# Pairing the 512-column and the 256-column products of the up projections

## What is computed

```python
def swiglu(u, w_in, w_out):
    a, b = jnp.split(u @ w_in, 2, axis=-1)          # 1024 -> 2 x 2816
    return (jax.nn.silu(a) * b) @ w_out
h = h + 0.5 * swiglu(rms_norm(h, ffn1_norm), ffn1_w_in, ffn1_w_out)   # ffn1, later ffn2
def squared_relu_mlp(h, w1, w2):
    return jnp.square(jax.nn.relu(h @ w1)) @ w2      # 1024 -> 4096, mlp0 and mlp1
```

## Time and profile before

| what | value |
|---|---|
| median of 3 runs | 1203.59 us |
| the profiled execution's own time | 1205.99 us |
| its span | 1204.2 us |
| TensorE busy | 1192.3 us (99%), 7787 matmuls |
| VectorE busy | 868.6 us (72%) |
| ScalarE busy | 646.5 us (54%) |
| GpSimd busy | 220.7 us (18%) |
| mean granted TensorE clock | 0.995 of full speed |

### The profile page before, as it was taken

One profiled execution on the slowest core, in us unless ns is written; L12 is line 12 of the kernel. 1 busy time (PEld: TensorE's weight loads), 2 busy tenths in 40 slices (PEclk: granted clock), 3 DMA queues, 4 the chain that ended last, 5 costly groups with the idle time before them and its releaser, 6 DMA issues.

```text
span 1204.2 us, 19499 instructions
## 1 busy us (share of the span) xinstructions
PE 1192.3 (99%) x7787; PEld 1063.5 (88%) x7787; DVE 868.6 (72%) x1199; ACT 646.5 (54%) x868; POOL 220.7 (18%) x110
## 2 busy tenths in 40 slices
PE   9999999999999999999999999999999999999997
PEld 6888888988899888888999988888899878888886
DVE  6877667788868877766788786665688777766553
ACT  6655544475655755545643554544446684555441
POOL 1443301000000234310000025410000240554000
PEclk9999999999999999999999999999999899999999
DMA  8545555952345555555545555555567204655540
GB/s 317 210 175 185 199 175 177 294 196 106 105 149 177 178 206 177 202 183 193 179 151 185 199 201 183 193 192 188 197 245 257 93 2 175 210 181 204 179 171 36
DMA packets 31569, 217.53 MB, mean 181 GB/s; under 512 B 3584, under 2 KB 3856, under 8 KB 6272
## 3 DMA queue, kind: packets, MB, share of 16 engines
q1 hardware_dynamic: 30000, 210.33, 49.7%
q0 software_dynamic: 1344, 5.53, 1.6%
q10 hardware_dynamic: 144, 0.52, 0.1%
HBM read 215.30 MB, written 4.22 MB: 182 GB/s over the span
## 4 chain that ended last, share of the span: by engine, by line
PE 98%; ACT 1%; DVE 1%; POOL 0%; issue 0%; DVEq 0%; ACTq 0%; POOLq 0%
PE bank L1546 42%; PE bank L1547 21%; PE bank L1539 8%; PE bank L1540 8%; PE bank L1541 8%; PE bank L1939 1%; PE bank L1647 1%; PE bank L1649 1%; PE bank L1648 1%; PE bank L1711 1%; PE bank L1833 0%; PE bank L1816 0%; PE bank L1986 0%; PE bank L1852 0%; PE bank L1655 0%; PE bank L2071 0%
## 5 line engine op out<-in xcount | busy, mean ns | idle before, releaser
L806 DVE TENSOR_TENSOR w_hl<-raw,w_hl 128x2048 fp32r<-128x2048 f32 x194 | 444.1, 2289 | 116.2 <-ACT w_hl L413 115.2
L413 ACT ACTIVATE w_hl<-raw 128x2048 fp32r<-128x2048 f32 x195 | 370.5, 1902 | 114.8 <-PE bank L1547 66.4
L1546 PE MATMUL bank<-x_hl,w_hl 128*128 128x512 f32 x912 | 319.9, 397 | 0.0
L1546 PE MATMUL bank<-hidden,w_hl 128*128 128x512 f32 x832 | 289.8, 395 | 0.0
L364 POOL TENSOR_TENSOR hidden<-hid_f,hidden 128x256 fp32r<-128x256 f32 (+1 forms) x76 | 189.6, 2494 | 521.6 <-ACT hidden L496 306.9
L1547 PE MATMUL bank<-x_hl,w_hl 128*128 128x256 f32 x912 | 254.2, 279 | 0.0
L1547 PE MATMUL bank<-hidden,w_hl 128*128 128x256 f32 x832 | 231.1, 278 | 0.0
L1546 PEld LDWEIGHTS bank<-x_hl,w_hl 128*128 128x128 f32 x912 | 171.2, 188 | 41.0
L1546 PEld LDWEIGHTS bank<-hidden,w_hl 128*128 128x128 f32 x832 | 156.1, 188 | 36.9
L1547 PEld LDWEIGHTS bank<-x_hl,w_hl 128*128 128x128 f32 x912 | 171.7, 188 | 0.1
L474 ACT ACTIVATE second<-bank 128x512 f32<-128x512 f32 (+1 forms) x107 | 57.1, 534 | 202.7 <-PE bank L1547 202.7
(11 more groups left out here) (371 smaller groups left out, 1534.1 us busy)
## 6 DMA issues: line engine op xcount, KB each, us to landing
raw<-weights SPq DMA_DIRECT2D x197, 1024.0 KB, 4.8
bias_skew<-bias_rows POOLq DMA_DIRECT2D x1, 3072.0 KB, 25.4
gate_or_bias<-bias_skew POOLq DMA_DIRECT2D x1, 2048.0 KB, 9.6
h<-x_t SPq DMA_DIRECT2D x2, 512.0 KB, 5.6
out_t<-out_g SPq DMA_DIRECT2D x4, 256.0 KB, 2.4
con<-consts SPq DMA_DIRECT2D x1, 769.5 KB, 12.6
raw<-weights ACTq DMA_DIRECT2D x1, 512.0 KB, 5.2
raw<-weights SPq DMA_DIRECT2D x1, 512.0 KB, 7.2
```

The lines of the kernel that those rows point to most:

```text
L413: nc.scalar.activation(dst, src, ACT.Copy).then_inc(hi_split, 1)
L806: V.tensor_tensor(w_lo[:, s, :], raw[:, s, :], w_hi[:, s, :].bitcast(F32), ALU.subtract).then_inc(lo_split, 1)
L1546: mm(out_, w_hi[:, s, c:c + m], x, start=start, stop=False, **kw)
```

## The change

`up` takes two tiles `k` of the model width at a time in the branch without pieces. A new helper, `two_wide`, issues both 512-column matmuls (high parts of the weights of k and k+1) and then both 256-column ones (low parts). So the order of widths goes from 512, 256, 512, 256 to 512, 512, 256, 256. The matmuls, their operands, the bank, the number of weight loads and the semaphores are as before; the first chunks of the stages, `up_halves`, the downs and the output projections are not touched.

```diff
+            def two_wide(out_, s, cs, m, xs, start, stop):
+
+                kw = dict(skip_group_check=True)
+                for n in range(2):
+                    mm(out_, w_hi[:, s, cs[n]:cs[n] + m], xs[n], start=start and n == 0, stop=False, **kw)
+                for n in range(2):
+                    last = mm(out_[:, 0:S], w_lo[:, s, cs[n]:cs[n] + m], xs[n][:, 0, :], start=False,
+                              stop=stop and n == 1, **kw)
+                return last
+
...
                 if pieces is None:
                     for t in range(2):
-                        for k in range(KT):
-                            last = wide(bank[:, 2 * slot + t, :], s, k * 256 + t * P, P, x[:, k, :, :], k == 0,
-                                        k == KT - 1)
+                        for k in range(0, KT, 2):
+                            last = two_wide(bank[:, 2 * slot + t, :], s, (k * 256 + t * P, (k + 1) * 256 + t * P), P,
+                                            (x[:, k, :, :], x[:, k + 1, :, :]), k == 0, k == KT - 2)
                     return last
```

## The result

The changed kernel takes 1210.9 us (median of 5 runs, 1208.58 to 1213.12) against 1203.89 us for the kernel before in the same comparison: a ratio of 1.0058, 95% interval 1.0037 to 1.0079, so 4.5 to 9.5 us slower. A later comparison (e1: 6 runs of the changed kernel, 27 of the kernel before) gave medians of 1208.96 and 1203.22 us, a ratio of 1.0050 (1.0030 to 1.0070). The forecast was 1200.9 us with a range of 1197.5 to 1209.2. Its sign is wrong in both comparisons. 1210.9 us lies outside the range; the median of e1 would lie just inside its upper end.

The account below looks back on a forecast made before the run. TensorE's own matmul rate was taken to bound the kernel. Gains of 2.1 us in ffn1's ups, 0 in other ups and 0.6 in ffn1's downs made 2.7 us, so 1203.6 - 2.7 = 1200.9 us, range 1197.5 to 1209.2.

Parts of the forecast that it names:

- The bound: Whole kernel: TensorE, busy 99% of the span, sets the time by its own rate of taking matmuls.
- always in time: Claim that operands, weights, banks and other engines never hold TensorE up; its ups have no waits.
- The quad in the ups: Two pairs in new order cost 693.3 ns, against 706.7 slow: 2.1 us gained in ffn1 ups, 0 in other ups.
- Whatever its neighbour: Steady TensorE stream: a matmul costs its columns and a fixed 13.3 ns, regardless of the adjacent matmul's width.
- The weight loads, banks, ends of chunks: In the changed ups: loads stay covered, banks and semaphores are released as before; costed at nothing.
- The downs: Untouched downs: ffn1's gain 1.2 us or 0, half taken, 0.6; the other stages' downs at nothing.
- each stage's downs have the rhythm of its ups: Rule read from the stretch table: slow in ffn1, 6.7 ns a pair over the other stages, in ups and downs alike.
- rival A: New order makes TensorE slow everywhere: 5.4 us in ups of ffn2, mlp0, mlp1, 1209.0 us; 1213.4 with downs; chance 0.28.
- a rest in its chances: Case where only later downs turn slow, up to 4.4 us; counted with most of the 0.28 for slower.
- The slow ffn1: ffn1's ups and downs run at a slow 353.3 ns a pair, the other stages at 346.7.

Follow-up runs that it names:

- e11: The kernel before, unaltered, profiled again; no time given; ffn1 changed rhythm on the way, 346.7 to 353.3 ns a pair.
- e7: Kernel before plus float32 256-column matmuls: one ahead of ffn1 and ffn2 downs, two ahead of mlp0 downs, one in mlp1 ups; 1210.25 us, one run.
- e8: Other orders of the ups, one per stage (eights, fours, quads over two banks, 512-256-256-512), downs in old order; 1209.24 us, ratio 1.0065 to kernel before.
- e2: Changed kernel with ffn1's last ups chunk in old order and a different extra matmul ahead of each other stage's downs; 1208.64 us, ratio 1.0050.
- e6: Changed kernel with an extra float32 matmul of 256 columns ahead of the downs of every stage; 1204.32 us, ratio 1.0015 to the kernel before.
- e9: Kernel before with chunk 2 of ffn1's ups in the new order and an extra float32 256-column matmul ahead of chunk 3; 1202.45 us, ratio 0.9999.
- e5: Kernel before with one extra float32 matmul of 256 columns ahead of chunk 3 of ffn1's ups; 1203.84 us, ratio 1.0013.

## Why the prediction was wrong

*The bound.* Right: TensorE's own rate decides, and the ups have no waits in the profiles before and after. (In e11 and e7 one wait of 0.3 and 0.2 us for weights stands in the ups of ffn1; the working said "always in time" from one execution.)

*The quad in the ups.* 693.3 ns was forecast, 696.7 measured, alike in all stages and in each of three profiles. Over 408 quads that is 1.3 us lost, over the 160 of ffn1 1.6 us gained against its slow rhythm instead of 2.1. Adding the steady costs of rows that hold one width only the earlier trace rows misses that each change of width disturbs the next few matmuls (e8); the miss is small. "Whatever its neighbour" was the wrong part of it.

*The weight loads, banks, ends of chunks.* Costed at nothing. e8 shows it for banks and operands: mlp0 and mlp1 took the same with other banks and another order of the same cycle.

*The downs.* This is the step that failed: "each stage's downs have the rhythm of its ups" was taken from the earlier trace rows as a rule, with the downs of ffn1 perhaps gaining (0.6 us in the sum) and the later downs at nothing. What the earlier trace rows show is that the old order handed on the old order's rhythm. The paired ups have another pattern, and what followed them was the slow rhythm in all 12 downs of three profiles. The downs of ffn1 gained nothing, and those of ffn2, mlp0 and mlp1 lost 1.2 + 1.7 + 1.5 = 4.4 us. Term by term the sum had -2.1 for the ups of ffn1, 0 for the other ups, -0.6 for the downs of ffn1 and 0 for the other downs, -2.7 us; the two profiles have -1.6, +1.3, 0.0 and +4.4, which is +4.1 us.

The 4.4 us were priced, but inside rival A, for the case that the ups turn slow too. Downs that turn slow behind ups that don't were named in the last paragraph of the prediction and, without a term or a price of their own, as a rest in its chances.

*Rival A.* Its sign was right, its place and price not. It was to decide where a quad costs over 693.3 ns on the mean; 696.7 is over that, but only a quarter of the way to the 706.7 of its price, 1.3 us of its 5.4. The rows that it rested on the earlier trace rows show 256-column matmuls ahead of the old order, and now two of them stand ahead of the downs. Read so, they spoke for slow downs, though a row of more than six there and a pair here are not the same entry.

*The slow ffn1.* The working took one execution's ffn1 for the kernel's. It is slow in three profiles of four (in four of five with e7), so the gain there exists only against those. Against a fast ffn1 the changed kernel loses 0.5 us in its ups and 1.2 in its downs. The terms that repeat are thus 1.3 + 4.4 us for ffn2, mlp0 and mlp1, and -1.6 to +1.7 us for ffn1: 4.1 to 7.4 us slower. Both measured intervals, 4.5 to 9.5 and 3.6 to 8.4 us, overlap with that.

*What stays open.* Why TensorE has these forms of one pattern, and what inside it they are, no run shows. The rule found is only about entries into the old order. A row of 256-column matmuls led to the slow form at all five places where one stands ahead of it, in all 17 profiles; paired ups did each time too, also with a bf16 matmul or a float32 one of 128 columns between (e2). The float32 matmul of 256 columns led from the slow form to a fast one in all 35 cases, and from the alternating fast form to the slow one in all seven. Behind paired ups its result depended on which of two quads it met (e6, e9). Its result is so fixed by the form and the place in it that it meets, as far as these traces go. Whether it acts by what it is or by the 0.24 us that it takes is not separated; a wait of 0.2 to 0.3 us for weights changed the form too (e11, e7). Why the mixer lost 3.1 us in one profile stays open too, beyond the late chunks.

## What to carry to other kernels

When one engine is busy all the time, measure its instructions from start to start, in every stage: the same code can run at two rates, and the list of mean lengths hides it. An edit to such a stream should be priced in what follows it as well as in itself. Where the trace has never seen what the edit puts ahead of the next stage, the slower of the known rhythms is the case to plan for there. And before a few us are read out of one profile, a second profile of the same kernel says which stretches repeat (here most to 0.01 us) and which don't.

## What the runs showed of the hardware

- A stream of 512- and 256-column float32r matmuls in turn has at least three steady forms: pairs of 353.3 ns (232 + 118, 241 + 120, 235 + 114 in turn), of 346.7 ns (233 + 117 and 231 + 112 in turn) and of 346.7 ns evenly (230 + 117). Each was seen to last for about a thousand matmuls (ups and downs of a stage) and over 100 us at a granted clock of 1.00, while VectorE, ScalarE and the DMA queues went on with their work.
- One instruction changes the form: a float32 matmul of 256 columns (e5, e6, e7), or a matmul that had to wait 0.17 or 0.28 us for its weights (e7, e11). The cost of the break itself, some 0.4 us, was less than what it switched (1.2 us in the downs of ffn1 and ffn2, 1.7 in those of mlp0, 1.5 in those of mlp1).
- The paired pattern had one form only, two alternating quads of 696.7 ns on the mean, reached in every stage of all three profiles of the changed kernel.
